# Gathering the tokens of four experts at a time, already turned, in a two-layer mixture-of-experts step

## What is computed

```python
def hier_moe(x, wg, bg, we, be, w1, w3, w2):
    # t = 384 tokens, dm = 1024; N_EXPERTS = 4 groups * 8; top-2 inside the best group
    g_sel = jnp.argmax(g_logits, axis=-1)
    top_v, top_i = lax.top_k(e_logits, TOP_K_IN_GROUP)
    weights = (jax.nn.softmax(top_v, axis=-1) * g_prob[:, None]).reshape(-1)
    eid = (g_sel[:, None] * EXPERTS_PER_GROUP + top_i).reshape(-1).astype(jnp.int32)
    ...
    def expert_block(args):
        xi, e = args
        hid = jax.nn.silu(xi @ w1[e]) * (xi @ w3[e])
        return hid @ w2[e]
    ...
    y = jax.ops.segment_sum(yb * slot_w[:, None], slot_tok, num_segments=t + 1)[:t]
```

## Time and profile before

| | us |
|---|---|
| median of 3 runs | 1768.45 |
| lowest, highest | 1767.39, 1774.14 |
| span of the profiled execution | 1768.3 |
| experts of layer 0, first hidden product to last copy | 437.8 to 913.2 |
| experts of layer 1, likewise | 1255.7 to 1733.6 |
| PE busy in the span | 1582.3 |
| DVE, ACT, POOL busy | 427.1, 301.4, 145.3 |

### The profile page before, as it was taken

The page is one execution under the profiler, slowest core; times in us unless marked ns, Lnnn a source line. Parts: engine busy times, 40 slices in busy tenths (PEclk is TensorE's granted clock), DMA queues, the critical chain, the costliest instruction groups (busy, mean ns, idle before and its releaser), DMA issues.

```text
span 1768.3 us, 21532 instructions
## 1 busy us (share of the span) xinstructions
PE 1582.3 (89%) x8498; PEld 781.0 (44%) x8498; DVE 427.1 (24%) x911; ACT 301.4 (17%) x606; POOL 145.3 (8%) x199
## 2 busy tenths in 40 slices
PE   4899876897999999999957998898899999999991
PEld 3454775644443333334423445654333333344440
DVE  0212275423311111111113022323411111111113
ACT  1100112411111111111112003431111111111112
POOL 1101103000000000000014000010000000000000
PEclk8899977697999999999987998998899999999996
DMA  9977944024999999999969422022499999999982
GB/s 352 256 255 258 347 179 161 1 75 166 372 423 423 424 424 423 424 423 424 423 278 303 159 95 84 1 76 113 179 419 423 424 424 423 423 424 424 423 372 110
DMA packets 99382, 522.15 MB, mean 295 GB/s; under 512 B 10090, under 2 KB 11562, under 8 KB 56320
## 3 DMA queue, kind: packets, MB, share of 16 engines
q1 hardware_dynamic: 85920, 485.58, 68.1%
q0 software_dynamic: 13408, 35.81, 6.4%
HBM read 511.60 MB, written 20.22 MB: 301 GB/s over the span
## 4 chain that ended last, share of the span: by engine, by line
PE 82%; DVE 6%; DMA 6%; ACT 3%; issue 2%; SPq 1%; POOL 0%; DVEq 0%; POOLq 0%; ACTq 0%
PE psum L827 24%; PE psum L517 14%; PE psum L840 12%; PE psum L808 9%; PE psum L773 5%; DMA ring<-in_moe_w 3%; PE psum L833 2%; PE psum L814 2%; PE psum L820 2%; PE psum L460 2%; PE psum L726 2%; PE psum L688 1%; PE psum L706 1%; ACT area_g L1091 1%; DMA ring<-in_ada_w 1%
## 5 line engine op out<-in xcount | busy, mean ns | idle before, releaser
L827 PE MATMUL psum<-ring,area_t 128*64 128x512 f32 x1024 | 450.1, 592 | 3.5 <-DMA ring<-in_moe_w 1.4
L828 PE MATMUL psum<-ring,area_t 128*64 128x512 f32 x1024 | 450.4, 593 | 0.0
L827 PEld LDWEIGHTS psum<-ring,area_t 128*64 128x64 f32 x1024 | 139.3, 137 | 292.8 <-issue 291.3
L517 PE MATMUL psum<-ring,area_t 128*128 128x512 f32 (+1 forms) x576 | 241.6, 581 | 0.0
L840 PE MATMUL psum<-ring,area_t 128*64 128x512 f32 x1024 | 235.5, 602 | 2.2 <-DVE area_t L1676 2.2
L808 PE MATMUL psum<-area_h,area_t 128*64 128x512 f32 x768 | 180.0, 604 | 3.0 <-DVE area_t L1661 3.0
L1647 DVE COPY area_q<-psum 64x512 f32<-64x512 f32 x64 | 44.5, 695 | 570.6 <-PE psum L828 570.5
L517 PEld LDWEIGHTS psum<-ring,area_t 128*128 128x128 f32 x576 | 110.0, 192 | 127.6 <-issue 125.8
L1853 POOL DMA_INDIRECT pair_rows<-area_q,idx x64 | 62.3, 973 | 940.3 <-ACT area_q L1137 925.7
L828 PEld LDWEIGHTS psum<-ring,area_t 128*64 128x64 f32 x1024 | 139.3, 137 | 0.0
L840 PEld LDWEIGHTS psum<-ring,area_t 128*64 128x64 f32 x1024 | 68.7, 137 | 120.5 <-issue 113.1
(11 more groups left out here) (238 smaller groups left out, 1363.0 us busy)
## 6 DMA issues: line engine op xcount, KB each, us to landing
ring<-in_moe_w SPq DMA_DIRECT2D x192, 2048.0 KB, 16.2
ring<-in_ada_w SPq DMA_DIRECT2D x24, 2048.0 KB, 16.9
ring<-in_na_w_in SPq DMA_DIRECT2D x6, 2048.0 KB, 18.0
ring<-in_ab_w_in SPq DMA_DIRECT2D x5, 2048.0 KB, 11.3
area_m<-mod_ready POOLq DMA_DIRECT2D x6, 1024.0 KB, 8.9
area_q<-pair_rows POOLq DMA_DIRECT2D x6, 1024.0 KB, 7.0
ring<-in_ab_w_out SPq DMA_DIRECT2D x2, 2048.0 KB, 15.6
area_g<-mod_ready POOLq DMA_DIRECT2D x4, 1024.0 KB, 7.7
```

Source lines behind the costliest of these rows:

```text
L517: mm = pe.matmul(banks[2 + g % 4][:, 0:w], hT[:, k, t * P:t * P + P], wchunk(n, KT)[:, k, 0:w], start=(k == 0), stop=(k == KT - 1))
L827: pe.matmul(banks[2 + u][0:64, :], lhsT, w1[:, k, :], start=(k == 0), stop=(k == KT - 1))
L828: mm = pe.matmul(banks[2 + u][64:128, :], lhsT, w3[:, k, :], start=(k == 0), stop=(k == KT - 1))
```

## The change

The work per expert is the same, but the tokens reach `xT` in another way and the loops go.

- **Gather.** `pick` now makes `sel4` for four experts at a time (for the first four: experts 0 and 1, then 2 and 3), one instruction per block of 128 tokens. PE's `gather` takes 128 x 128 pieces of `h`, every fourth column, as the stationary operand and `sel4` as the moving one, so the tokens come out turned: `tokens`, ACT's copy to `tok`, and the four turnings of `turn_tokens` are gone. A group of four experts takes four blocks `gather(l, q, g)`, each of 2 pieces x 3 token tiles with 256 columns. In the first group a block has 4 pieces x 3 tiles with 128 columns, and two blocks make two experts. Which block stands behind which expert's hidden products is in `GATHERS`.
- **Places.** The rows to scatter to are found once per layer: DVE's `rank_slots` makes a matrix for each of a token's two choices, PE's `places` multiplies them with `val`, and DVE's `index` writes `idx` with a column per expert. `index_products` per expert is gone, but for the overflow branch.
- **Loops.** The expert loops of SP, PE, ACT and DVE are written out. PE's order is now hidden(e), the gather blocks of `GATHERS[e]`, after expert 0 `places`, turn_hidden(e), down(e).

```diff
+        sel4 = [area_t[:, 768 * i:768 * i + 768].rearrange("p (t e s) -> p t e s", t=NT, e=4) for i in range(2)]
+        xT4 = [area_q[:, 5120 + 2048 * i:7168 + 2048 * i].rearrange("p (k s) -> p k s", k=KT) for i in range(2)]
+        slots = area_q[:, 3352:4120].rearrange("p (k t s) -> p k t s", k=2, t=NT)
...
+        QUADS = EXPERTS // 4
+        PICKS = QUADS + 1
+        def turned(l, q, g):
+            return l * EXPERTS + 4 * q + g + 1
+        GATHERS = {0: ((0, 2),), 1: ((0, 3), (1, 0)), 2: ((1, 1), (1, 2)), 3: ((1, 3),)}
+        for _e in range(4, EXPERTS - 4):
+            GATHERS[_e] = ((_e // 4 + 1, _e % 4),)
+        for _e in range(EXPERTS - 4, EXPERTS):
+            GATHERS[_e] = ()
...
             def load_experts(l):
-                base = NUM["moe", l, 0]
-                def one(e, u):
+                for e in range(EXPERTS):
                     for j in range(3):
-                        at = place(base + 3 * u + j)
-                        dst = expert_dst(ring[:, at, :], j)
-                        if isinstance(e, int) and e < 2:
-                            freed(sp, base + 3 * e + j - RING)
-                        else:
-                            sp.wait_ge(M["y_done"] if j == 2 else M["hid_done"], e + (l * EXPERTS - 1))
-                        sp.dma_start(dst, expert_dram(l, e, j)).then_inc(landed[at], 16)
-                one(0, 0)
-                one(1, 1)
-                with sp.Fori(1, EXPERTS // 2) as i:
-                    for u in range(2):
-                        one(sp.snap(i * 2 + u), u)
+                        n = NUM["moe", l, 3 * e + j]
+                        load(n, expert_dst(ring[:, place(n), :], j), expert_dram(l, e, j))
...
-            def tokens(e, u, base):
-                pe.wait_ge(M["sel_ready"], e + (base + 1))
-                if not (isinstance(e, int) and e + base < 1):
-                    pe.wait_ge(M["tok_copied"], e + base)
-                token_products([(sel[u][:, t, :], t) for t in range(NT)]).then_inc(M["tok_done"], 1)
-            def turn_tokens(e, u, base):
-                if not (isinstance(e, int) and e + base < 1):
-                    pe.wait_ge(M["index_ready"], e + base)
-                column = [val[:, t, e:e + 1] if isinstance(e, int) else val[:, t, bass.ds(e, 1)] for t in range(NT)]
-                index_products([(sel[u][:, t, :], column[t]) for t in range(NT)]).then_inc(M["index_done"], 1)
-                pe.wait_ge(M["tok_copied"], e + (base + 1))
-                if not (isinstance(e, int) and e + base < 1):
-                    pe.wait_ge(M["xT_copied"], e + base)
-                token_turns().then_inc(M["xT_done"], 1)
-            def hidden(e, u, base, w1, w3):
-                pe.wait_ge(M["xT_copied"], e + (base + 1))
-                if not (isinstance(e, int) and e + base < 2):
-                    pe.wait_ge(M["silu_done"], e + (base - 1))
-                    pe.wait_ge(M["up_copied"], e + (base - 1))
-                hidden_products(u, w1, w3).then_inc(M["hid_done"], 1)
-            def turn_hidden(e, u, base):
-                pe.wait_ge(M["silu_done"], e + (base + 1))
-                pe.wait_ge(M["up_copied"], e + (base + 1))
-                if not (isinstance(e, int) and e + base < 1):
-                    pe.wait_ge(M["hidT_ready"], e + base)
+            def gather(l, q, g):
+                pe.wait_ge(M["sel_ready"], l * PICKS + (1 + g // 2 if q == 0 else 2 + q))
+                n = 4 * (QUADS * l + q) + g
+                if n >= 2:
+                    pe.wait_ge(M["xT_copied"], n - 1)
+                if q == 0:
+                    ks, cols = range(4 * (g % 2), 4 * (g % 2) + 4), slice(2 * (g // 2), 2 * (g // 2) + 2)
+                else:
+                    ks, cols = range(2 * g, 2 * g + 2), slice(0, 4)
+                w = 64 * (cols.stop - cols.start)
+                for i, k in enumerate(ks):
+                    first = 512 * (k // 4) + k % 4
+                    for t in range(NT):
+                        mm = pe.matmul(banks[n % 2][:, w * i:w * i + w], h[:, t, first:512 * (k // 4) + 512:4],
+                                       sel4[q % 2][:, t, cols, :].rearrange("p e s -> p (e s)"),
+                                       start=(t == 0), stop=(t == NT - 1))
+                mm.then_inc(M["xT_done"], 1)
...
+            def places(l):
+                pe.wait_ge(S["slots_ready"], l + 1)
+                for k in range(2):
+                    for t in range(NT):
+                        mm = pe.matmul(banks[5][:, 0:EXPERTS], slots[:, k, t, :], val[k][:, t, :],
+                                       start=(k == 0 and t == 0), stop=(k == 1 and t == NT - 1))
+                mm.then_inc(S["places_done"], 1)
...
+                gather(l, 0, 0)
+                gather(l, 0, 1)
+                for e in range(EXPERTS):
+                    ns = [NUM["moe", l, 3 * e + j] for j in range(3)]
+                    ws = [wchunk(ns[j], 4 if j == 2 else KT) for j in range(3)]
+                    for j in range(2):
+                        pe.wait_ge(landed[place(ns[j])], when(ns[j]))
+                    hidden(l, e, ws[0], ws[1])
+                    for q, g in GATHERS[e]:
+                        gather(l, q, g)
+                    if e == 0:
+                        places(l)
+                    turn_hidden(l, e)
+                    pe.wait_ge(landed[place(ns[2])], when(ns[2]))
+                    down(l, e, ws[2])
...
-                stt(val, o2, 2.0, last(keep[:, KEEP["pair"]], EXPERTS), ALU.mult, ALU.add)
-                for k in range(2):
+                for k, oh in enumerate((o1, o2)):
                     ts(pval[:, k, :], keep[:, KEEP["pair"]], 2.0 * k, None, ALU.add)
...
+            def rank_slots(l):
+                for k, (oh, rank) in enumerate(((o1, m1), (o2, m2))):
+                    tt(c32, oh, key, ALU.mult)
+                    red(rank, c32, ALU.add)
+                    tt(slots[:, k, :, :], lead(keep[:, KEEP["slot"]], NT), last(rank, P), ALU.is_equal,
+                       "dve_step" if k == 0 else "slots_ready")
...
+            def turn(l, q, g):
+                n = 4 * (QUADS * l + q) + g
+                v.wait_ge(M["xT_done"], n + 1)
+                if q >= 2:
+                    v.wait_ge(M["hid_done"], l * EXPERTS + 4 * (q - 1))
+                if q == 0:
+                    dst = xT4[0][:, 4 * (g % 2):4 * (g % 2) + 4, 128 * (g // 2):128 * (g // 2) + 128]
+                    src = banks[n % 2][:, :].rearrange("p (k s) -> p k s", k=4)
+                else:
+                    dst = xT4[q % 2][:, 2 * g:2 * g + 2, :]
+                    src = banks[n % 2][:, :].rearrange("p (k s) -> p k s", k=2)
+                v.tensor_copy(dst, src).then_inc(M["xT_copied"], 1)
+            def pick(l, e0, e1):
+                q = e0 // 4
+                if q >= 2:
+                    v.wait_ge(M["xT_done"], turned(l, q - 2, 3))
+                n = e1 - e0
+                for t in range(NT):
+                    ins = v.tensor_tensor(sel4[q % 2][:, t, e0 - 4 * q:e1 - 4 * q, :],
+                                          lead(keep[:, KEEP["slot"]][:, 0:BLOCK], n), last(key[:, t, e0:e1], BLOCK),
+                                          ALU.is_equal)
+                ins.then_inc(M["sel_ready"], 1)
+            def index(l):
+                v.wait_ge(S["places_done"], l + 1)
+                do(v.tensor_scalar(idx[:, :], banks[5][:, 0:EXPERTS], keep[:, KEEP["skip"]], None, ALU.add),
+                   "places_ready")
...
+                pick(l, 0, 2)
+                pick(l, 2, 4)
+                pick(l, 4, 8)
+                for g in range(2):
+                    turn(l, 0, g)
+                rank_slots(l)
+                for e in range(EXPERTS):
+                    one(l, e)
+                    product(l, e)
+                    for q, g in GATHERS[e]:
+                        turn(l, q, g)
+                    if e % 4 == 0 and e // 4 + 2 < QUADS:
+                        pick(l, e + 8, e + 12)
+                    if e == 0:
+                        index(l)
+                        weigh(l)
...
+                pool.wait_ge(S["places_ready"], l + 1)
                 for e in range(EXPERTS):
-                    scatter(M, e, e % 2, base, l)
+                    scatter(M, e, e % 2, base, l, idx[:, e:e + 1])
```

188 lines of the change are left out of this document (61 added, 127 removed).

## The result

| | before | after |
|---|---|---|
| median, us (lowest to highest) | 1768.04 (1767.39 to 1774.14) | 1827.24 (1824.91 to 1830.67) |
| span of the profiled execution | 1768.3 | 1826.0 |
| layer 0, first hidden product to last copy | 437.8 to 913.2 (475.4) | 435.2 to 938.4 (503.2) |
| layer 1, likewise | 1255.7 to 1733.6 (477.9) | 1288.6 to 1791.6 (503.0) |
| PE busy | 1582.3 | 1558.4 |

The change makes the kernel slower: ratio 1.034, 95% interval 1.0319 to 1.0362, about 59 us. The forecast was 1782, with a range of 1766 to 1800.

What follows compares the result with a forecast made beforehand. The prediction took the DMA weight-chunk chain to set each stage's end. A start 2.5 us later plus DMA idling in experts 0 to 2 made it 7.2 us late: 1768.3 + 2 x 7 = 1782.3, forecast 1782, range 1766 to 1800.

Steps and rivals of the forecast that it cites:

- Mid-stage gives nothing for the passes removed: Per expert, the removed 1.23 us of PE passes only filled a wait that stays; gain none, PE's period stays 14.84 us.
- The weighing behind expert 0 still ends before expert 1's rows are turned.: Behind expert 0, DVE's weighing was claimed to finish before PE turns expert 1's hidden rows; no loss was counted.
- The strided load, 0.142 us a pass, hidden under 0.214: Gather's every-fourth-column load of h: limits 128-column passes at 0.142 us, hides under 256-column passes of 0.214 us.
- the unhidden case, 12 x 0.235, +0.25 us per expert: Mid-stage gather block if the strided load does not hide under 256-column passes: +0.25 us per expert, left out of the sum.
- Start +2.5, first experts +8.0: Each layer: stage start +2.5 us (bounds +1.4 and +3.8); experts 0 to 2 together +8.0 us of PE.
- DMA's chain carries the early loss to the end: From expert 5's first chunk on, DMA's chain stays full, so its 7.2 us lateness per layer reaches the stage's end.
- The ring's reserve lasts to expert 31: Kernel before: PE loses nothing to slower DMA until the six-chunk weight ring's reserve runs out just before the end.
- The loops written out: 0: Expert loops written out give nothing by themselves: no pass is late across a loop's turn at 600 to 616 us.
- Rival C: Written-out loops add instruction fetches on DMA, one engine up to 12 us late per layer: 1788 to 1806, chance 0.15.
- The end of a stage: Experts 28 to 30 have no gather: 5.5 us less PE, but DMA decides expert 31; layer 7 us longer.
- rival D: Idle PE ahead of down products lowers the clock, 5.35 instead of 3.65 us, in half the experts: 1790 to 1830, chance 0.05.
- the forecast's own term, 14: Both layers' later DMA chain, 2 x 7 us, from the longer start and DMA idling in experts 0 to 2.

Runs made afterwards that it cites:

- the filler run: Kernel after, with eight unread 128-column passes between turning the hidden rows and the down products for experts 2 to 31: 1831.67 us, ratio to before 1.0362.
- the places alone: Kernel before, with scatter rows found once per layer and the six column passes per expert gone: 1773.7 us, ratio 1.0017.
- the run with both repairs: Kernel after, with the pick for experts 8 to 11 moved behind expert 1 and gather loading adjacent columns (wrong row order): 1789.87 us, ratio to before 1.0119.

## Why the prediction was right or wrong

The sign was right and the size wrong: +14 forecast, +59 measured. By its steps:

- **Mid-stage gives nothing for the passes removed.** Right. The wait is 1.60 us with and without filling (the filler run), the places alone moved the time by no more than their interval (1.0017).
- **"The weighing behind expert 0 still ends before expert 1's rows are turned."** This is the step that failed most, 22 of the 59 us. I took the length of the work (10 us) and not its place behind a wait. The diff has the order: `turn`, then `pick(l, e + 8, e + 12)`, then `index`, `weigh`, and the pick waits for `turned(l, q - 2, 3)`, that is block (0, 3), which `GATHERS` puts behind expert 1. DVE runs in order, so everything behind it waits for PE to come to expert 1's gather, and PE waits for a copy behind that. Naming what is queued behind each added wait would have found it; I did that for POOL's wait and not for DVE's.
- **The strided load, 0.142 us a pass, hidden under 0.214.** This term failed too. The mechanism was named, its price mis-sized: 0.24 us, 329 ns a load, and not hidden under 256 columns. I even had "the unhidden case, 12 x 0.235, +0.25 us per expert", which came true (+0.22), and dropped it. This is 16 of the 59 us. The row it was taken from, the turnings, is one pass a tile; the gather's products are two passes a tile, with loads of 190 ns to begin with.
- **Start +2.5, first experts +8.0.** In the run with both repairs 2.3 and 8.2 in layer 0, but 0.7 and 6.4 in layer 1, and the agreement in layer 0 is in part luck. At the start two errors cancel: PE was at the half clock for about 4.9 us (0.50 to 431, 0.74 from 431 to 433, 1.00 from 433) and not 3.0, and a pass at the full clock took 0.116 us and not 0.142. In the first experts, expert 0's down products took 5.35 us instead of 3.65 in layer 0, 1.7 us that the sum didn't have; in layer 1 they took 3.65. In the kernel after, with the strided load, the start is +5.9.
- **DMA's chain carries the early loss to the end.** Right in the repaired kernel (the run with a third of the first group's gather took back 7 to 9 us per layer for 7.7 us of PE, and both have the hidden products 15.15 us apart in the last experts). In the kernel after the loss is so large that PE sets the pace up to expert 30, which I had expected of DMA; at expert 31 they meet.
- **The ring's reserve lasts to expert 31.** Read too late: in the kernel before PE already waits 0.44 us for a chunk before expert 28 of layer 0. It changes nothing in the sum.
- **The loops written out: 0.** Too low; the run gave +6 [+2, +11]. Rival C had fetch packets as the mechanism, which no run moved alone, and priced it at up to 12 us a layer; up to expert 31 the layers lost 3.7 and 1.6.
- **The end of a stage.** I had 3 x 1.84 us less PE. The period there is 13.04 us, 2.0 under the new 15.06; but two of the last four experts' down products take 5.35 us, 1.7 more each (the granted clock from 891.5 to 895.5 is 0.57, a part of it at 1.2 GHz). That is rival D in the small. The filler took the half clock away without a gain, since PE then waited 1.9 us for expert 31's chunk.

With the sizes measured, the account is 22 (DVE's order) + 16 (strided loads) + 22 (what is left with both repairs, 1789.87 - 1767.75) = 60, against 59 measured. Of the last, 6 belong to the loops, if they cost the same here as in the kernel before, and the 16 that remain are the forecast's own term, 14. My range ended at 1800 since no case in it had two faults at once, and since the one it needed most, a wait on DVE, wasn't among the rivals.

## What to carry to other kernels

On an engine that runs in order, a moved step is as late as the last wait in front of it: for each new wait write down which engine satisfies it and behind which of its own waits, and follow that once around the circle. A stationary tile of float32 was cheap to load with a step of one or two elements and not of four; lay the data out once, outside the loop. When DMA bounds a stage, its time is set by when its chain starts, so microseconds ahead of the first freed buffer go to the end nearly in full, and microseconds of PE in the middle are waited for at the end; here the cheapest gain was to keep PE busy in the waits just ahead. And before a trace is read for the effect of a change, look at how much the same rows differ between executions of kernels without it.

## What the runs showed of the hardware

- A 128 x 128 float32 load of a product took 190 ns with adjacent columns, 197 with every second, 329 with every fourth; of a turning, 140 with adjacent columns and 202 with every fourth. With 128 columns to stream a pass took 0.116 us with the 190 ns load and 0.24 with that of 329.
- The strided pass doesn't get faster with the clock. In windows of the kernel after, 423 to 430 us at a mean granted clock of 0.68 hold 31 gather passes in 7.00 us, with the loads on PEld busy for all of it; at 1.00 (442 to 448) a block of 24 took 5.87: 0.23 and 0.24 each. In the run with both repairs (second fence), with adjacent columns, it is 18 passes in 3.85 us at 0.50, 0.21 each, and 0.116 each at 1.00.

```profile
423.00:430.00 7.00, 7.00 (x31) 7.00 (x31) 2.09 (x6) 0.00 (x0) 0.00 (x0) 0.68 0.00 0
```

```profile
427.00:431.00 4.00, 3.85 (x18) 3.85 (x19) 1.71 (x7) 0.00 (x0) 0.00 (x0) 0.50 0.00 0
```

- The sixteen passes of an expert's down products took 3.65 us or 5.35, after 1.0 us of idle ahead of both; with the idle filled those of experts 2 to 31 all took 3.65.
- With the loops written out there were 31 more instruction packets, and the chunks of a full DMA landed 5.09 us apart instead of 5.04 to 5.06.
